# Three products of every weight block in another order, with two successive products on one stationary tile and the wait for the low part at the head of each piece

## The reference

```python
# first block
proj = einsum('bsd,dc->bsc', rmsnorm(x), w_in)              # 2048 x 8200
h = x + einsum('bsc,cd->bsd', y, w_out)                     # 2048 x 2048
e = einsum('bsr,rd->bsd', p, w_pe)                          # 256 x 2048
gate = sigmoid(einsum('bsd,de->bse', rmsnorm(h), w_pg))     # 2048 x 2048
x = rmsnorm(h + gate * e)
# second block
proj = rmsnorm(x) @ w_in_2                                  # 2048 x 9216
merged = sigmoid(g_a) * (y_a @ w_up_a_2) + sigmoid(g_b) * (y_b @ w_up_b_2)   # 1024 x 2048, twice
x = x + merged @ w_o_2                                      # 2048 x 2048
hid = rmsnorm(x) @ w_ffn_in_2                               # 2048 x 11264
x = x + (silu(gate) * up) @ w_ffn_out_2                     # 5632 x 2048
x = x + sigmoid(rmsnorm(x) @ w_ple_gate_2) * (p_2 @ w_ple_2)
```

## Time and profile before

| | |
|---|---|
| time, median of 3 runs | 2066.08 us (2065.88 to 2068.45) |
| profiled execution, first to last instruction (span) | 2066.0 us |
| PE busy (matmuls) | 2053.2 us, 9445 matmuls |
| PEld busy (weight loads) | 1703.5 us, 9445 loads |
| DVE busy | 1221.1 us |
| ACT busy | 976.4 us |
| mean granted TensorE clock | 0.999 of full speed |

### The profile page before, as it was taken

One profiled execution on the slowest core, in us unless ns is written; L12 is line 12 of the kernel. 1 busy time (PEld: TensorE's weight loads), 2 busy tenths in 40 slices (PEclk: granted clock), 3 DMA queues, 4 the chain that ended last, 5 costly groups with the idle time before them and its releaser, 6 DMA issues.

```text
span 2066.0 us, 24467 instructions
## 1 busy us (share of the span) xinstructions
PE 2053.2 (99%) x9445; PEld 1703.5 (82%) x9445; DVE 1221.1 (59%) x1304; ACT 976.4 (47%) x1221; POOL 34.0 (2%) x44
## 2 busy tenths in 40 slices
PE   8999999999999999999999999999999999999999
PEld 7888888888888888888888888888888888888887
DVE  5877776555666665655455554555555555555664
ACT  6545445544565456444444444344434443444453
POOL 1000000000001100000000000000000000000000
PEclk9999999999999999999999999999999999999999
DMA  8544354556556554455555555555555555555553
GB/s 278 169 139 162 128 199 143 190 184 210 190 183 204 183 164 162 163 183 189 197 183 196 181 175 197 188 184 189 195 183 185 191 192 183 190 192 187 183 184 122
DMA packets 191772, 377.09 MB, mean 183 GB/s; under 512 B 8482, under 2 KB 10196, under 8 KB 191572
## 3 DMA queue, kind: packets, MB, share of 16 engines
q1 hardware_dynamic: 191700, 376.10, 55.3%
HBM read 373.98 MB, written 2.10 MB: 182 GB/s over the span
## 4 chain that ended last, share of the span: by engine, by line
PE 97%; DVE 1%; ACT 1%; issue 0%; DMA 0%; SPq 0%; DVEq 0%; ACTq 0%
PE acc L854 61%; PE acc L859 31%; PE aux L837 2%; PE aux L918 1%; PE aux L828 1%; DVE wlo L1283 0%; DMA resid<-in_x 0%; PE aux L908 0%; PE aux L933 0%; DVE att_z L1783 0%; PE aux L1106 0%; PE aux L1116 0%; PE aux L1143 0%; DVE att_l L1781 0%; ACT whi L506 0%
## 5 line engine op out<-in xcount | busy, mean ns | idle before, releaser
L1283 DVE TENSOR_TENSOR wlo<-raw,whi 128x1024 fp32r<-128x1024 f32 x704 | 860.3, 1224 | 779.4 <-ACT whi L506 775.4
L506 ACT ACTIVATE whi<-raw 128x1024 fp32r<-128x1024 f32 x704 | 745.4, 1060 | 1051.0 <-PE acc L859 1039.7
L854 PE MATMUL acc<-whi,actA_hi 128*128 128x512 f32 x1472 | 581.2, 395 | 1.2 <-DVE actA_lo L1298 1.2
L854 PE MATMUL acc<-whi,actA_lo 128*128 128x512 f32 x1472 | 575.2, 391 | 0.0
L859 PE MATMUL acc<-wlo,actA_hi 128*128 128x512 f32 x1472 | 394.5, 390 | 0.0
L854 PEld LDWEIGHTS acc<-whi,actA_hi 128*128 128x128 f32 x1472 | 277.6, 189 | 58.2 <-DVE actA_lo L1298 1.6
L854 PE MATMUL acc<-whi,actB_hi 128*128 128x512 f32 x828 | 325.0, 393 | 0.0
L859 PEld LDWEIGHTS acc<-wlo,actA_hi 128*128 128x128 f32 x1472 | 277.1, 188 | 57.7
L854 PEld LDWEIGHTS acc<-whi,actA_lo 128*128 128x128 f32 x1472 | 277.9, 189 | 55.6
L854 PE MATMUL acc<-whi,actB_lo 128*128 128x512 f32 x828 | 322.5, 389 | 0.0
L859 PE MATMUL acc<-wlo,actB_hi 128*128 128x512 f32 x828 | 221.8, 390 | 0.7 <-DVE wlo L1283 0.6
(11 more groups left out here) (268 smaller groups left out, 1156.5 us busy)
## 6 DMA issues: line engine op xcount, KB each, us to landing
raw<-in_w_in SPq DMA_DIRECT2D x132, 1024.0 KB, 5.1
raw<-in_w_ffn_in SPq DMA_DIRECT2D x88, 1024.0 KB, 5.0
raw<-in_w_ffn_out SPq DMA_DIRECT2D x44, 1024.0 KB, 5.1
raw<-in_w_out SPq DMA_DIRECT2D x16, 1024.0 KB, 5.2
raw<-in_w_pg SPq DMA_DIRECT2D x16, 1024.0 KB, 5.2
raw<-in_w_o SPq DMA_DIRECT2D x16, 1024.0 KB, 5.1
raw<-in_w_ple_gate SPq DMA_DIRECT2D x16, 1024.0 KB, 5.2
raw<-in_w_up_a SPq DMA_DIRECT2D x8, 1024.0 KB, 5.1
```

What stands on the lines that cost most here:

```text
L506: act.activation(whi[:, g % RING], raw_piece(g), ACT.Copy).then_inc(hi_ready, 1)
L854: pe.matmul(acc2(n)[:, t, :], act[x][:, k + c, t * P:(t + 1) * P], whi[:, g % RING, c, :], start=(p == 0 and c == 0 and x == 0), stop=False)
L1283: dve.tensor_tensor(wlo[:, g % RING], raw_piece(g), whi[:, g % RING].bitcast(F32), ALU.subtract)\
```

## The change

The two loops of `piece` become one. For each block `c` and each token half `t`, the three products now stand together, in the order low activation by high weight, high activation by high weight, high activation by low weight. The second and the third have the same stationary tile, `act[0]` of that block and half. The wait for `hi_ready` is gone; the wait for `lo_ready`, which stood ahead of the ninth matmul, stands ahead of the first. (`lo_ready` of a piece implies its `hi_ready`, since VectorE waits for that itself.) No other engine's instructions change.

```diff
-                pe.wait_ge(hi_ready, g + 1 + i * ROUND)
-                for c in range(PK):
-                    for t in range(T):
-                        for x in range(2):
-                            pe.matmul(acc2(n)[:, t, :], act[x][:, k + c, t * P:(t + 1) * P], whi[:, g % RING, c, :],
-                                      start=(p == 0 and c == 0 and x == 0), stop=False)
                 pe.wait_ge(lo_ready, g + 1 + i * ROUND)
                 for c in range(PK):
                     for t in range(T):
-                        ins = pe.matmul(acc2(n)[:, t, :], act[0][:, k + c, t * P:(t + 1) * P], wlo[:, g % RING, c, :],
-                                        start=False, stop=(last and c == PK - 1))
+                        o = acc2(n)[:, t, :]
+                        for x, w in ((1, whi), (0, whi), (0, wlo)):
+                            ins = pe.matmul(o, act[x][:, k + c, t * P:(t + 1) * P], w[:, g % RING, c, :],
+                                            start=(p == 0 and c == 0 and x == 1), stop=(last and c == PK - 1 and w is wlo))
                 ins.then_inc(piece_used, 1)
```

## The result

The changed kernel takes 2072.93 us (median of 6 executions, 2072.21 to 2075.59) against 2066.82 us of before (6 executions, 2065.88 to 2068.45): 6.1 us more, a ratio of 1.003 with a 95% interval from 1.0019 to 1.0042. The profiled execution has a span of 2070.9 us. The time of an execution is 1.7 us above its span in all of them (2072.65 for this one), so the profiled execution of before, with its span of 2066.0, was not one of 2066.1 us but one of about 2067.7. Executions of one kernel fall into two groups some 2.4 us apart (of before: 2065.3 to 2066.0 and 2067.6 to 2068.4), and which of them holds a median is chance; the profile of before is one of the upper group, the one of the changed kernel one of the lower.

The account below looks back on a forecast made before the run. The prediction took TensorE's matmuls, 2053.2 of 2066.0 us, as the bound. Pairs 0 plus waits 1.2 + 0.6 + 1.8 + 1.8 + 0.1 = 5.5 us on 2066.1 gave 2071.6 us, range 2067.5 to 2076.

Parts of the forecast that it names:

- The pairs: In each piece, 4 second products repeat a stationary tile, 2812 in all; their loads stay, so the change is 0 us.
- a rival of 31 us: The second product of each pair comes 11 ns sooner, 31 us gained, giving 2040.6 us with the waits; 12 in 100.
- bounds of 37 us gained and 19 lost: Over 2812 pairs: 37 us gained if the load's 13.3 ns vanish, 19 lost if a low tile loaded under `wlo` costs 6.7.
- 20 ns of actM: Matmuls with tiles in actM or hidT stand 233 ns apart, 20 ns beyond the 213.3 ns of streaming 512 columns.
- the 13 ns: Matmuls in other pieces stand 226.7 ns apart, 13 ns beyond the 213.3 ns of streaming 512 columns.
- Piece 0: First piece: its head waits for VectorE's split, 1.2 us; about 0.6 if the clock rises at the same moment as before.
- Piece 73: Its split follows the convolution: a new wait of 0.5 us and 0.1 for a load not hidden, together 0.6 us.
- Pieces 241 and 261: VectorE's split is late: heads move by 2.08 and 2.59 us, less 0.27 and 0.78 paid before, net 1.81 each.
- Piece 259: The split ends just before the head, leaving 0.09 us, but the load starts some 0.2 us ahead: 0.1 us taken.
- Nothing won back: Behind all the delayed pieces TensorE is the bound again, with no later wait that a delay could fill.
- the clock rival: The clock falls once or twice behind the stand-stills of 2.1 and 2.6 us, some 1.6 us each: 2073.2 or 2074.8; 11 in 100.

Follow-up runs that it names:

- experiment 2: The changed kernel once more, no edit, for a second profile of the clock: 2073.31 us, against 2066.04 us of before.
- experiment 1: The kernel before, in its old product order, with only the wait for `lo_ready` moved to each piece's head: 2072.76 us, against 2067.83 us of before.

## Why the prediction was right

By its own steps:

- **The pairs are worth nothing.** Taken as 0, with a rival of 31 us and bounds of 37 us gained and 19 lost. Right, and shown: two profiles that differ in order alone end 0.03 us apart (experiment 2), and every matmul kept its load. Of the 20 ns of actM, which I took as speaking for the rival, 6.7 went away when tiles were moved, with every load still made; whether it is the load or the streaming that a place slows is not shown. That a load of the tile already present is not skipped follows from the counts; what the 13 ns are stays open. The rule of the Trainium skill that the prediction weighed ("TensorE: Matmul & The Clock Gate", Part 2: the next load runs under the present matmul) fits this result, since repeating a tile won nothing; its 216 ns for 512 columns were not reached by any float32r product here, 226.7 ns being the distance in most pieces and the shortest of the two classes.
- **Piece 0, taken as 1.2, between 0.6 and 1.2.** The head moved by 1.27 us in the first profile. The clock rose where it had risen before, at 13.8 us, and only 0.66 us remained, the lower bound. In the second profile it rose at 16.7 us and the second piece began 2.0 us later than in before's profile, over my upper bound. The moment of the rise differs from profile to profile: 12.1 to 14.6 us in the eight profiles with the old wait at piece 0, 13.8 to 16.7 in the five with the wait at its head. So this term depends on more than the wait, and my 1.2 was not measured in either profile.
- **Piece 73, taken as 0.6.** Measured 0.52 + 0.13 = 0.65.
- **Pieces 241 and 261, taken as 1.8 each.** Measured at 241: head 2.08 later, 0.27 won back at the ninth matmul, 1.81. At 261, where the clock didn't fall there (experiments 1 and 2): head 2.51 and 2.56 later than at piece 260, 0.75 and 0.79 won back, so 1.76 and 1.77.
- **Piece 259, taken as 0.1.** No wait of a matmul is recorded there, but the matmuls of the piece stand up to 0.24 us apart instead of 0.227, and the next piece starts 0.08 us later (0.03 to 0.08 in the four profiles with the whole wait at the head and the tail where it was). Right in size.
- **Nothing won back.** Right: in the profile of the changed kernel the distance to before is 4.95 us at piece 262 and 4.94 at the last one.
- **The clock.** This is the term that was left out of the sum and put among the rivals with 11 in 100. It fell behind one of the two long stand-stills in both profiles of the changed kernel and in that of experiment 1, and behind nothing at these places in the other ten. Its price is about what the rival said ("some 1.6 us", although 6 matmuls of 0.227 us, by its own count, are 1.4): at 261 in the first profile the piece lost 1.5 us more than the wait explains, at 241 in the other two 1.6.

The sum, by the first profile: the waits cost 0.66 + 0.65 + 1.81 + 0.08 + 1.76 = 5.0 us, the fall behind piece 261 another 1.5, together 6.5. Before's own profile has the fall near 304 us, 1.6 us, which this one lacks, and so the two end 4.9 us apart. The lower groups stand some 7 us apart (2072.2 to 2073.4 against 2065.3 to 2066.0); the rest beyond 6.5 is of the size that the moment of the first rise moves, which no run separates. The medians differ by 6.1, since before's median is itself a mixture of both groups.

The forecast of 5.5 us was thus right in mechanism and place. Its closeness to 6.1 is in part luck: in the first profile the waits alone came out at 5.0, with piece 0 at half of what I took, and the clock's fall, which the sum left out, made up for more than that. The median of 2072.93 us lies nearer to the 2073.2 of the clock rival than to the 2071.6 of the sum, and what that rival describes is what the profiles show. I had given it 11 in 100, and it came in all three profiles that have both long stand-stills.

## What to carry to other kernels

Before a wait is moved ahead of work that does not need it, list for every instance the lead of what it waits for, not the median: here 698 of 703 pieces had enough, and of the five that did not, the two that had been waiting already paid the whole time of the work that the wait passed. Repeating a stationary tile saved nothing here, where each matmul brought its own load. A stand-still of TensorE can cost a second time in its clock; reordering the late engine and putting independent matmuls into the hole both cured it here.

## What the runs showed of the hardware

- A float32r matmul with 512 moving columns usually stood 226.7 ns after the one before it when its stationary and its moving tile lay alike modulo 512 bytes in the partition (by places worked out, not recorded), and 232.5 to 233.3 ns in the three arrangements where they did not. Order and repeated tiles made no difference to that. Modulo 256 would fit the same runs. In every kernel some of the pieces stood wider than this.
- The clock's fall is tied to the stand-still, but not to its length alone: in two profiles it fell behind the 2.1 us at piece 241 and not behind the 2.5 us at piece 261, in a third the other way round. In the profile where the clock had risen at 13.8 us, it fell behind 261; in the two where it had risen at 16.7 us, behind 241. What decides it was not tried.
- The fall near 304 us, behind small plain float32 matmuls, came in the profiles of before, of experiments 1 and 2, of the new order with `wlo` early and of the kernel with all tensors moved, and in no other. Where it can be read by comparison it cost some 1.6 us. All five of these profiles are executions of their kernel's upper group, and the eight without it are of the lower, so it makes 1.6 of the 2.4 us between the groups. I take the moment of the first rise for the rest, which no run shows by itself.
